# Two layer norms whose statistics move into the product before them, and expert weight loads that are split between two issuing engines

## The reference

```python
def first_block(x, ...):
    h = x
    for layer in range(DEPTH):
        ...
        h = layer_norm(ALPHA * h + mix, ln_mix_g[layer], ln_mix_b[layer])
        ffn = hierarchical_moe(h, moe_w_group[layer], moe_w_expert[layer], moe_w13[layer], moe_w2[layer])
        h = layer_norm(ALPHA * h + ffn, ln_ffn_g[layer], ln_ffn_b[layer])
    return h

def layer_norm(x, g, b):
    mu = jnp.mean(xf, axis=-1, keepdims=True)
    var = jnp.mean(jnp.square(xf - mu), axis=-1, keepdims=True)
    return ((xf - mu) * lax.rsqrt(var + LN_EPS) * g + b).astype(x.dtype)

    def expert_block(args):                     # in hierarchical_moe, on blocks of rows of one expert
        xb, e = args
        hcat = xb @ w13[e]
        hid = jax.nn.silu(hcat[:, :EXPERT_FF]) * hcat[:, EXPERT_FF:]
        return hid @ w2[e]
```

## Time and profile before

| | us |
|---|---|
| median of 3 runs | 3633.75 |
| lowest and highest of them | 3625.1 and 11575.98 |
| the profiled execution, its own time | 3637.38 |
| its span in the trace | 3635.6 |
| TensorE busy | 3197.6 (88%) |
| VectorE busy | 985.1 (27%) |
| ScalarE busy | 770.0 (21%) |
| DMA, mean over the span | 176 GB/s |

### The profile page before, as it was taken

One profiled execution on the slowest core, in us unless ns is written; L12 is line 12 of the kernel. 1 busy time (PEld: TensorE's weight loads), 2 busy tenths in 40 slices (PEclk: granted clock), 3 DMA queues, 4 the chain that ended last, 5 costly groups with the idle time before them and its releaser, 6 DMA issues. The chain is left out here.

```text
span 3635.6 us, 39606 instructions
## 1 busy us (share of the span) xinstructions
PE 3197.6 (88%) x16263; PEld 1629.9 (45%) x16263; DVE 985.1 (27%) x1980; ACT 770.0 (21%) x1592; POOL 240.5 (7%) x228
## 2 busy tenths in 40 slices
PE   8998997987775998788777759999999989999999
PEld 4447963332221446333222225565644435556444
DVE  2425633200002106230000030166500211176202
ACT  1412251100001005110000033245500013245200
POOL 0015410000000000100000011100000001100000
PEclk9998988999898999889898879999999999999999
DMA  6431413999998532379999841111011111121121
GB/s 205 173 122 59 203 48 154 417 427 415 399 392 329 207 139 48 105 292 427 420 407 396 365 139 35 53 39 47 24 47 46 58 46 39 47 46 47 47 80 48
DMA packets 168838, 639.58 MB, mean 176 GB/s; under 512 B 63476, under 2 KB 65906, under 8 KB 142672
## 3 DMA queue, kind: packets, MB, share of 16 engines
q1 hardware_dynamic: 151440, 576.27, 41.4%
q0 software_dynamic: 8576, 29.26, 2.3%
q10 hardware_dynamic: 8640, 31.46, 2.1%
HBM read 584.38 MB, written 56.50 MB: 176 GB/s over the span
## 5 line engine op out<-in xcount | busy, mean ns | idle before, releaser
L1534 PE MATMUL banks<-weight_ring,experts_xT 128*32 128x512 f32 (+1 forms) x2240 | 386.1, 642 | 92.0 <-DMA weight_ring<-in_moe_w 76.9
L2524 PE MATMUL banks<-weight_ring,cols 128*128 128x512 f32 x672 | 294.4, 600 | 14.2 <-PEq L2663 8.2
L1552 PE MATMUL banks<-weight_ring,experts_hT 128*32 128x512 f32 (+1 forms) x1216 | 247.8, 642 | 44.6 <-DMA weight_ring<-in_moe_w 43.7
L1534 PEld LDWEIGHTS banks<-weight_ring,experts_xT 128*32 128x32 f32 (+1 forms) x2240 | 117.5, 124 | 303.0 <-issue 250.0
L2524 PE MATMUL banks<-weight_ring 128*128 128x512 f32 x480 | 207.0, 593 | 3.7 <-PEq L2502 1.9
L2524 PEld LDWEIGHTS banks<-weight_ring,cols 128*128 128x128 f32 x672 | 128.7, 192 | 178.4 <-issue 178.4
L1534 PE MATMUL banks<-cols,experts_xT 128*32 128x512 f32 (+1 forms) x640 | 188.4, 649 | 21.2 <-DMA cols<-in_moe_w 16.8
L1534 PE MATMUL banks<-experts_slot,experts_xT 128*32 128x512 f32 (+1 forms) x448 | 177.9, 666 | 25.0 <-DMA experts_slot<-in_moe_w 25.0
L1552 PE MATMUL banks<-cols,experts_hT 128*32 128x512 f32 (+1 forms) x448 | 170.6, 639 | 16.9 <-DMA cols<-in_moe_w 16.9
L3032 PE MATMUL banks<-cols,weight_ring 128*128 128x512 f32 x416 | 182.9, 592 | 1.9 <-PEq L282 1.9
L672 PE MATMUL banks<-cols,weight_ring 128*128 128x512 f32 x384 | 170.4, 599 | 1.1 <-PEq L282 1.1
(11 more groups left out here) (439 smaller groups left out, 4429.7 us busy)
## 6 DMA issues: line engine op xcount, KB each, us to landing
weight_ring<-in_moe_w SPq DMA_DIRECT2D x132, 2048.0 KB, 19.6
cols<-in_moe_w SPq DMA_DIRECT2D x40, 2048.0 KB, 24.8
experts_slot<-in_moe_w SPq DMA_DIRECT2D x20, 2048.0 KB
weight_ring<-in_w_in SPq DMA_DIRECT2D x16, 2048.0 KB, 7.9
weight_ring<-in_w_ada SPq DMA_DIRECT2D x12, 2048.0 KB, 11.4
weight_ring<-in_a_w_in SPq DMA_DIRECT2D x8, 2048.0 KB, 12.0
block_rows_out<-experts_y ACTq DMA_DIRECT2D x32, 512.0 KB, 10.8
experts_xin<-block_rows_in ACTq DMA_DIRECT2D x28, 512.0 KB, 16.5
```

What stands on the lines that cost most here:

```text
L1534: mm = pe.matmul(bank[a:a + n, :], self.xT[:, 4 * part + k, a:a + n], slots(r, part)[:, k, c:c + 512], start=part == k == 0, stop=part == ...
L1552: mm = pe.matmul(self.out[c][a:a + n, :], self.hT[:, f, a:a + n], slots(r, 2)[:, f, c * 512:c * 512 + 512], start=f == 0, stop=f == 3)
L2524: mm = pe.matmul(ps[i % 8][0:u.shape[0], 0:u.shape[1]], u.lhs(w, k), u.rhs(w, k), start=k == 0, stop=k == u.kd - 1)
```

## The change

Two things are changed.

First, the statistics of the two layer norms behind the mixers are made where the rows are made. After each of the eight residual additions VectorE makes the statistics of that half row, and after the second half of a tile it aggregates them into `K.row_mv`. `stage_layer_norm` begins with the wait for gain and bias.

Second, the 27 expert pieces of a layer whose place is freed by a `down` (`behind_down`) are taken out of SyncE's list. ScalarE issues them, one to three at a time, right behind its store of the rows of that `down`. SyncE's list keeps its order without them. The engine that loads a piece of an expert for the first time also reads the expert's number, so for such experts two engines now read it.

```diff
@@ stage_layer_norm
-        V, S = K.steps("layer_norm", dve=[f"{x}{t}" for t in range(NT) for x in ("st0", "st1", "mv")]
-                       + [f"c{t}" for t in range(NT)] + [f"n{t}" for t in range(NT)], act=["ln", "rs"])
+        V, S = K.steps("layer_norm", dve=[f"c{t}" for t in range(NT)] + [f"n{t}" for t in range(NT)], act=["ln", "rs"])
...
             def _(dve):
-                for t in range(NT):
-                    dve.bn_stats(st[:, t, 0, :], X[:, t, 0:512]).then_inc(*V(f"st0{t}"))
-                    dve.bn_stats(st[:, t, 1, :], X[:, t, 512:1024]).then_inc(*V(f"st1{t}"))
-                    dve.wait_ge(*V.at(f"st1{t}"))
-                    dve.bn_aggr(mv[:, t, :], st[:, t, :, :]).then_inc(*V(f"mv{t}"))
                 dve.wait_ge(K.loaded, K.n_loaded)
                 for t in range(NT):
-
-                    dve.wait_ge(*V.at(f"mv{t}"))
...
             def _(act):
-                act.wait_ge(*V.at(f"mv{NT - 1}"))
@@ stage_dn_recurrence
                     dve.scalar_tensor_tensor(K.H[:, t, n], x[:, t, n], ALPHA, ps[banks[units.index((g, t)) % 4]], ALU.mult,
                                              ALU.add).then_inc(*V(f"e{g}{t}"))
+                    dve.wait_ge(*V.at(f"e{g}{t}"))
+                    dve.bn_stats(stats[:, g, :], K.H[:, t, n]).then_inc(*V(f"b{g}{t}"))
+                    if g == 1:
+                        dve.wait_ge(*V.at(f"b1{t}"))
+                        dve.bn_aggr(K.row_mv[:, t, :], stats[:, :, :]).then_inc(*V(f"mv{t}"))
+                        dve.wait_ge(*V.at(f"mv{t}"))
@@ residual_take
+        dve.wait_ge(*done.at((g, t, "sum")))
+        if g == 0:
+            dve.bn_stats(stats[:, t, g, :], dst).then_inc(*inc)
+        else:
+            dve.bn_stats(stats[:, t, g, :], dst).then_inc(*done.up((g, t, "stats")))
+            dve.wait_ge(*done.at((g, t, "stats")))
+            dve.bn_aggr(K.row_mv[:, t, :], stats[:, t, :, :]).then_inc(*inc)
@@ stage_experts
+        behind_down = {m: LAST_USE[m - MOE_SLOTS][1] for m in range(MOE_SLOTS, 3 * NE) if LAST_USE[m - MOE_SLOTS][0] == "down"}
+
+        def load_weights(eng, m, expert):
+            r, part = LOADS[m]
+            if r not in expert:
+                eng.wait_ge(*V.at("order"))
+                expert[r] = eng.value_load(X.order[0:1, r:r + 1], min_val=0, max_val=NE - 1)
+            if m % MOE_SLOTS == MOE_SLOTS - 1 and m < MOE_SLOTS:
+                eng.wait_ge(*E.at("logits"))
+            if m >= MOE_SLOTS:
+                eng.wait_ge(*B.passed(*LAST_USE[m - MOE_SLOTS]))
+            src, k, w = expert_load(K, l, expert[r], part)
+            eng.dma_start(slots(r, part), src).then_inc(own[m % MOE_SLOTS], 16)
...
                 for m in range(RING, 3 * NE):
-                    r, part = LOADS[m]
...
-                    sp.dma_start(slots(r, part), src).then_inc(own[m % MOE_SLOTS], 16)
+                    if m not in behind_down:
+                        load_weights(sp, m, expert)
...
                     if p:
                         B.store_y(act, p - 1)
+                        for m, q in behind_down.items():
+                            if q == p - 1:
+                                load_weights(act, m, expert)
```

More of the change, by code:

```diff
@@ L142, in __init__ @@
         self.lam = nc.alloc_sbuf_tensor("lam", [P, 2], F32)
+        self.row_mv = nc.alloc_sbuf_tensor("row_mv", [P, NT, 2], F32)
         self.ng = nc.alloc_sbuf_tensor("norm_g", [P, DEPTH, KD], F32)
@@ L1151, in stage_dn_recurrence @@
     pe_labels += [f"T{NT - 1}" if u == "turn" else f"u{u[0]}{u[1]}" for u in order]
-    dve_labels += [f"F{NT - 1}"] + [f"e{u[0]}{u[1]}" for u in units]
+    dve_labels += [f"F{NT - 1}"] + [x for g, t in units for x in [f"e{g}{t}", f"b{g}{t}"] + [f"mv{t}"] * g]
     act_labels += [f"T{NT - 1}"]
@@ L1323, in _, with residual_take @@
                                              ALU.add).then_inc(*V(f"e{g}{t}"))
-def residual_take(K, H):
-    def take(dve, u, bank, inc):
-        c = u[0] * 512 + u[3]
-        dst = H[:, u[2], c:c + 512]
-        dve.scalar_tensor_tensor(dst, dst, ALPHA, bank, ALU.mult, ALU.add).then_inc(*inc)
+                    dve.wait_ge(*V.at(f"e{g}{t}"))
[4 more added lines that the diff above has]
+                        dve.wait_ge(*V.at(f"mv{t}"))
+def residual_take(K, H, stats):
+    done = Tally(K, "layer_norm_dve", [(g, t, x) for g in range(2) for t in range(NT) for x in ["sum"] + ["stats"] * g])
+    def take(dve, u, bank, inc):
+        g, t = u[0], u[2]
+        dst = H[:, t, g * 512 + u[3]:g * 512 + u[3] + 512]
+        dve.scalar_tensor_tensor(dst, dst, ALPHA, bank, ALU.mult, ALU.add).then_inc(*done.up((g, t, "sum")))
+        dve.wait_ge(*done.at((g, t, "sum")))
[5 more added lines that the diff above has]
+            dve.bn_aggr(K.row_mv[:, t, :], stats[:, t, :, :]).then_inc(*inc)
     return take
@@ L1705, in _ @@
                 for m in range(RING, 3 * NE):
-                    r, part = LOADS[m]
-                    if r not in expert and len(expert) == FIXED:
-                        sp.wait_ge(*V.at("order"))
-                    if r not in expert:
-                        expert[r] = sp.value_load(X.order[0:1, r:r + 1], min_val=0, max_val=NE - 1)
-                    if m % MOE_SLOTS == MOE_SLOTS - 1 and m < MOE_SLOTS:
-                        sp.wait_ge(*E.at("logits"))
-                    if m >= MOE_SLOTS:
-                        sp.wait_ge(*B.passed(*LAST_USE[m - MOE_SLOTS]))
-                    src, k, w = expert_load(K, l, expert[r], part)
-                    sp.dma_start(slots(r, part), src).then_inc(own[m % MOE_SLOTS], 16)
+                    if m not in behind_down:
+                        load_weights(sp, m, expert)
                 sp.wait_ge(*B.passed("down", NP - 1))
@@ L1827, in _ @@
                     act.activation(K.lam[:, 0:2], K.lam[:, 0:2], ACT.Exp).then_inc(*S("lam"))
+                expert = dict(enumerate(range(FIXED)))
                 for p in range(NP):
@@ L2382, in differential @@
         stage_to_cols(K, "diff_out_cols", O, K.OT, NT, scale=w[:, 0, :], shift=w[:, 1, :])
-    with nc.sbuf_tensor("rpb_wide", [HEADS * RPB_R, DEPTH, 127], F32) as wide:
-        stage_gemm(K, "diff_out", [("rows", KD, 512)] * 2, K.OT, NT, None, residual_take(K, K.H),
+    with nc.sbuf_tensor("rpb_wide", [HEADS * RPB_R, DEPTH, 127], F32) as wide, nc.sbuf_tensor("out_stats", [P, NT, 2, 6], F32) as stats:
+        stage_gemm(K, "diff_out", [("rows", KD, 512)] * 2, K.OT, NT, None, residual_take(K, K.H, stats),
                    beside=expand_rpb(K, wide))
```

5 lines of the change are left out of this document (3 added, 2 removed).

## The result

| | before | after |
|---|---|---|
| median of 19 runs each, us | 3630.96 | 3616.88 |
| ratio after to before, 95% interval | | 0.9967 [0.9959, 0.9976] |
| the profiled execution, its own time | 3637.38 | 3618.19 |
| its span | 3635.6 | 3616.4 |

The change makes the kernel faster by 0.33%, 12 us of 3631 (interval 9 to 15). The forecast was 3640, a little slower than before: the time moved the other way. The two profiled executions differ by 19 us, but 5.5 us of that lie ahead of anything that the change touches: the product before the first layer norm ends at 595.2 instead of 600.7, at a granted clock of 1.00 instead of 0.94 from 500 to 590 us. So I compare stages and not the whole spans.

A forecast was written before the change was run, and what follows sets the result against it. The prediction took expert weight loads by DMA to bound the expert passes. It summed 3637.4 + 0.9 (statistics) + 4 (expert part) = 3642.3 us, 3638.7 on the median's scale, and predicted 3640 us, range 3630 to 3652 (chance 0.50).

The forecast's parts named there:

- What bounds the kernel: Expert passes: weight loads by DMA bound the stage, not a compute engine; the last of 96 pieces sets its end.
- Statistics: Layer norms: the load of gain and bias replaces the statistics as the wait; +0.9 us, bounds 0 and +1.8.
- The issue on ScalarE: Expert passes: issuing pieces takes ScalarE 1 to 3 us in a pass, in otherwise idle time; price 0.
- The dry moments: Expert passes: times when DMA engines lack work because a `down` wait holds back pieces; removing most gains 15 to 20 us.
- the 33 us of missing rate: Expert passes, both layers: the most that running at the full 428 GB/s could win.
- the 512 KB transfers: Expert passes: transfers said to stay and to account for the rest of the 33 us beyond the dry moments.
- The forecast rate of 408 to 415 GB/s: Expert passes: the DMA rate expected in the windows of 400 us after the change.
- rival 1: Expert passes: the dry moments go and nothing replaces them, 3618 us; sign a rate above 420; chance 0.22.
- The late input rows: Expert passes: input rows queue behind ScalarE's pieces and land late; naive sum 23 us in a layer, mostly given back.
- Pieces that share the engines: Expert passes: pieces needed later share engines with urgent ones, making new dry moments; nothing to about 10 us per layer.
- the sum of the expert part: Expert passes: gain and costs together, taken as +4 us for both layers, between -33 and +66 us.
- Rival 2: Expert passes: late input rows stall TensorE and delay the freeing of places; 12 us a layer, 3662 us, chance 0.18.

The follow-up runs named there:

- e1: The changed kernel with the expert stage of the kernel before, so only the statistics are moved: 3628.55 us, ratio 1.000 to the kernel before.
- e10: The changed kernel with layer 1's gain and bias loaded early and SyncE issuing each layer's last six pieces in order of need: 3594.56 us, ratio 0.9913.
- e4: The changed kernel, but ScalarE issues the load of the input rows ahead of the weight pieces: 3615.27 us, ratio 0.9959 to the kernel before.
- e5: The changed kernel, but SyncE issues the last six pieces, in the order 91, 92, 90, 93, 94, 95: 3608.43 us, ratio 0.9930.
- e3: The changed kernel, but SyncE issues all pieces, sorted by when their place comes free, and ScalarE none: 3627.81 us, ratio 0.9995.
- e7: The changed kernel with gain and bias of both layer norms loaded early, during the product before: 3617.33 us, ratio 0.9958 to the kernel before.
- e6: e3 with the last six pieces in the order 91, 92, 90, 93, 94, 95: 3612.72 us, ratio 0.9945 to the kernel before.

## Why the prediction was wrong

- **What bounds the kernel**: right. What e1 to e10 moved counted where it changed when the last packet lands, what stands behind it, or, in layer 1, when the stage begins.
- **Statistics, +0.9 us**: right. Layer 0 measured +1.06 us, layer 1 -0.07, both released by the bias, with waits of 6.33 and 8.09 us where 5 and 8 were forecast.
- **The issue on ScalarE, 0**: right. ScalarE is busy for 28.6 us of 400, and its three issues in a row take 3.2 us, as forecast; in the passes TensorE waits for ScalarE's work 1.9 us in each layer, as before.
- **The dry moments, -15 to -20 us**: the mechanism was right and the size too small. The last packet comes 29 us sooner in the two layers. I had the 33 us of missing rate in hand and put half of it down to "the 512 KB transfers, which stay". The window of after has the same transfers and runs at 425 to 427: they cost at most 1 to 3 GB/s. The forecast rate of 408 to 415 GB/s is wrong for the same reason; the prediction's own sign for rival 1, a rate above 420, is what came. Three moments picked by eye were a poor measure of a sum for which a window had the number.
- **The late input rows, naively 23 us in a layer**: the rows were late about as forecast (31.4 us to land, forecast 36; 56.6 us of waits, forecast 46 in two layers), and cost nothing that the runs can show. e4 takes away 51 of those 56.6 us and the time moves by 3 us, inside the intervals. I had written that most of it is given back, and then let the count of them pull the sum above zero all the same.
- **Pieces that share the engines, up to 10 us in a layer**: a cost of that size is there, and lies in one place that the text didn't name, the tail: 7.5 and 9.0 us, of which e5 takes away 4.1 and 7.3 by a change to the last six pieces alone. In the passes no such cost is seen, since the windows run at the full rate. And e3 has the long tail with one queue of pieces: it is less the sharing between two queues than that pieces with a later need go ahead.
- **The step that failed** is the sum of the expert part, "I take +4 us for both layers together", and in it two terms: the dry moments, put at -15 to -20 us, were -29.0, and the late input rows, which were to lift the sum a little above zero, were 0. The term that was left open between nothing and 20 us, pieces in the wrong order, was 16.5. With the terms as measured the sum is -29.0 + 16.5 + 0 = -12.5 us. Rival 1 (the dry moments go, 3618 us) had the time by luck: it said that nothing replaces them, and a larger gain met a cost that it left out.
- **Rival 2** needed TensorE's stalls to push back the points that free places. TensorE does stall, by up to 8.0 us each time, and it doesn't matter while the engines have pieces left to load: without the stalls (e4) the last packet comes 0.3 us later and 0.4 us sooner. In e7 the same mechanism does decide, for one stall of 18.56 us.

In the passes the engines' full rate with two queues (425 to 427) is that of one queue (428 in the earlier trace rows). That agrees with the rule of the Trainium skill, page "DMA: Bandwidth & Descriptors", section "Rules for kernel authors", that issuing from several engines brings no bandwidth. But the rule says that it saves issue time only, and here the last packets came 29 us sooner in another way: SyncE's wait at the head of its list held back the pieces behind it, and the second list has a place of its own to wait. e6 shows that a better order in one queue buys much of the same.

## What to carry to other kernels

When a queue issues transfers that wait for places, sort it by the point at which each place comes free, or give those with late points a queue of their own; but at the end of the stage sort by need, since what counts there is how much work stands behind the last packet. Size the gain of the rate by the window's rate against the best rate seen, not by a few gaps picked out. A wait of a compute engine cost nothing here while the DMA engines that bound the stage stayed full, and starting a step earlier can cost, as in e7, if it puts its urgent small transfers beside a backlog that would have been through: look at both layers, or both ends, before keeping it.

## What the runs showed of the hardware

- A transfer in small packets does badly beside weight pieces. The scatter (4 KB packets, 4.17 MB) took 29.4 us in the changed kernel, 644.7 to 674.1, and 48.6 us in e7, 638.5 to 687.1, where a full backlog stood beside it; 1.42 against 4.16 MB in the same 13 us. Nearly alone it moved 1.89 MB in 5 us, 378 GB/s. ScalarE's stores show it too: the one of 2031.4 to 2037.7 us needed 6.3 us for 0.52 MB beside SyncE's pieces. The Trainium skill, page "DMA: Bandwidth & Descriptors", section "Queues, rings and completion order", says that each DMA engine goes round between its queues by packets; the bytes that the two queues moved, one against three, agree with packets of 4 KB against 16 KB (one against four).
- Between two queues with pieces of one size the engines were shared evenly, 3.49 and 3.33 MB from 917 to 933 us in the changed kernel. The half that the prediction took for it holds. The 3.36 and 2.61 MB of 2032 to 2046 us are less even because ScalarE's queue has the store's small packets until 2037.7; from 2038 to 2046 it is 1.49 MB of SyncE's and 1.92 of ScalarE's. The split from 917 to 933 us, columns as above:

```profile
q1 hardware_dynamic: 229, 3.49, 51.3%
q10 hardware_dynamic: 224, 3.33, 48.8%
```

- After TensorE's stall of 18.56 us in e7 its granted clock was 0.78 in 690 to 700 us, a mix of its two levels (1.2 and 2.4 GHz), against 1.00, the upper one, in the same window of the changed kernel.
